# A mixture-of-experts entry on Trainium2: gate weights' low half first, block table later, first down weights beside the first gathers

## What is computed

```python
def hier_moe(x, ...):
    # every token chooses one of 4 groups, and in it 2 of 8 experts, each with a weight
    # pairs (token, weight) are listed by expert; an expert works on blocks of 128 rows
    def expert_block(args):
        xblk, e = args
        hidden = jax.nn.silu(xblk @ w_g[e]) * (xblk @ w_u[e])
        return hidden @ w_d[e]
    # the rows of each block, times their weights, are added to their tokens
```

## Time and profile before

| | us |
|---|---|
| median of 3 runs | 1715.81 (1714.29 to 1717.73) |
| the profiled execution | 1714.82 |
| its span, first to last instruction | 1713.0 |
| TensorE busy | 1665.4 (97%) |
| TensorE's weight loads busy | 1463.1 (85%) |
| VectorE busy | 1264.9 (74%) |
| ScalarE busy | 930.4 (54%) |
| GpSimd busy | 248.8 (15%) |

### The profile page before, as it was taken

One profiled execution on the slowest core, in us unless ns is written; L12 is line 12 of the kernel. 1 busy time (PEld: TensorE's weight loads), 2 busy tenths in 40 slices (PEclk: granted clock), 3 DMA queues, 4 the chain that ended last, 5 costly groups with the idle time before them and its releaser, 6 DMA issues.

```text
span 1713.0 us, 24990 instructions
## 1 busy us (share of the span) xinstructions
PE 1665.4 (97%) x9010; PEld 1463.1 (85%) x9010; DVE 1264.9 (74%) x2101; ACT 930.4 (54%) x1184; POOL 248.8 (15%) x269
## 2 busy tenths in 40 slices
PE   8999999999999999999999999999999999999994
PEld 7999987777999999879998888888888888888882
DVE  5234799986766667655464558999889899889886
ACT  6363121216433344426343337887878778788785
POOL 4100111110000000011001123511111212122111
PEclk9999999999999999999999998999999999999998
DMA  5402223231243233366343339999999999999975
GB/s 203 145 26 75 75 100 107 94 108 57 93 142 105 93 93 93 102 199 214 117 166 129 105 105 373 390 394 380 383 378 384 377 382 371 377 381 381 384 276 221
DMA packets 103171, 367.26 MB, mean 214 GB/s; under 512 B 14628, under 2 KB 58872, under 8 KB 88240
## 3 DMA queue, kind: packets, MB, share of 16 engines
q1 hardware_dynamic: 79824, 308.76, 48.2%
q0 software_dynamic: 23056, 57.36, 10.3%
q10 hardware_dynamic: 208, 0.08, 0.0%
HBM read 326.24 MB, written 61.22 MB: 226 GB/s over the span
## 4 chain that ended last, share of the span: by engine, by line
PE 72%; PEld 15%; DMA 4%; DVE 3%; ACT 2%; issue 2%; DVEq 1%; SPq 0%; ACTq 0%; PEldq 0%; POOLq 0%
PE bank L1069 68%; PEld bank L1069 15%; PE bank L1524 2%; DMA wraw_down<-in_w_expert_down 1%; DMA wraw_up<-in_w_expert_up 1%; PE bank L1548 1%; DMA uo<-in_x_prompt 1%; DVE gwork L2107 1%; PE bank L1441 0%; DMA h_scr<-ybuf,kdT 0%; ACT L1641 0%; PEld bank L1288 0%; DMA s<-in_state_gla 0%; DMA wraw_gate<-h_scr 0%; DVE wraw_gate L2674 0%
## 5 line engine op out<-in xcount | busy, mean ns | idle before, releaser
L2107 DVE TENSOR_TENSOR wL_down<-wraw_down,wH_down 128x1024 fp32r<-128x1024 f32 x140 | 162.0, 1218 | 25.6 <-ACT wH_down L1641 25.1
L2107 DVE TENSOR_TENSOR wL_up<-wraw_up,wH_up 128x2048 fp32r<-128x2048 f32 x72 | 161.6, 2285 | 21.6 <-ACT wH_up L1641 21.6
L2107 DVE TENSOR_TENSOR wL_gate<-wraw_gate,wH_gate 128x2048 fp32r<-128x2048 f32 x72 | 161.7, 2287 | 12.1 <-ACT wH_gate L1641 12.1
L1641 ACT ACTIVATE wH_up<-wraw_up 128x2048 fp32r<-128x2048 f32 x72 | 134.0, 1909 | 66.2 <-DMA wraw_up<-in_w_expert_up 51.8
L2232 DVE SCALAR_TENSOR_TENSOR ybuf<-uo,gwork,ybuf 128x1024 f32<-128x1024 f32 x120 | 154.5, 1288 | 6.1 <-issue 6.1
L1641 ACT ACTIVATE wH_down<-wraw_down 128x1024 fp32r<-128x1024 f32 x140 | 136.6, 1051 | 18.5 <-DMA wraw_down<-in_w_expert_down 18.4
L1641 ACT ACTIVATE stage<-bank 128x512 f32<-128x512 f32 (+3 forms) x65 | 34.5, 546 | 190.2 <-PE bank L1069 180.8
L997 POOL DMA_INDIRECT h_scr<-ybuf,kdT x34 | 77.1, 2269 | 399.7 <-ACT ybuf L1641 360.9
L1641 ACT ACTIVATE wH_gate<-wraw_gate 128x2048 fp32r<-128x2048 f32 x72 | 134.5, 1934 | 1.2 <-DMA wraw_gate<-in_w_expert_gate 1.2
L1069 PE MATMUL bank<-nTH,gateH 128*128 128x352 f32 x384 | 129.5, 337 | 0.7 <-issue 0.6
L1069 PE MATMUL bank<-nTH,slabH 128*128 128x352 f32 x384 | 124.9, 325 | 1.2 <-ACT uo L1641 0.7
(11 more groups left out here) (359 smaller groups left out, 4279.5 us busy)
## 6 DMA issues: line engine op xcount, KB each, us to landing
wraw_gate<-in_w_expert_gate SPq DMA_DIRECT2D x36, 2048.0 KB, 19.1
wraw_up<-in_w_expert_up SPq DMA_DIRECT2D x36, 2048.0 KB
wraw_down<-in_w_expert_down SPq DMA_DIRECT2D x36, 2048.0 KB
slab_raw<-in_w_in SPq DMA_DIRECT2D x7, 2048.0 KB, 9.6
gate_scr<-stage POOLq DMA_DIRECT2D x16, 528.0 KB, 3.6
vr_scr<-stage POOLq DMA_DIRECT2D x32, 256.0 KB, 2.3
gate_raw<-in_w_in SPq DMA_DIRECT2D x16, 512.0 KB, 8.7
vrbuf<-vr_scr SPq DMA_DIRECT2D x16, 512.0 KB, 6.9
```

Source lines behind the costliest of these rows:

```text
L1641: return act.activation(out, in_, func, **kw)
L2107: return dve.tensor_tensor(out, x, y, op)
```

## The change

On SyncE's queue the down weights of block 0 go ahead of the wait for gather 0, and the up weights of block 1 wait for gather 1 too. On VectorE the low halves of block 0 go ahead of the count and the weight list, and the table of further blocks is made after block 2 instead of before block 0; the two steps that take up the table move two blocks later. On TensorE four fillers go ahead of the last token list; sixteen fillers stand between the list and the first transposes (there were two); the weight list and the count come after those transposes, then two fillers (there were eight). On GpSimd, gathers 3 and 4 and scatter 0 go ahead of the table. The loops of TensorE and VectorE begin at block 6 instead of block 4.

```diff
@@ SyncE
             load_w(sp, W_UP, 0, 0)
             load_w(sp, W_GATE, 1, 1)
+            load_w(sp, W_DOWN, 0, 0)
             sp.wait_ge(xg_loaded[0], 16)
-            load_w(sp, W_DOWN, 0, 0)
+            sp.wait_ge(xg_loaded[1], 16)
             load_w(sp, W_UP, 1, 1)
@@ GpSimd
             gather(2)
+            gather(3)
+            gather(4)
+            scatter(0)
             pool.wait_ge(more_made, 1)
...
-            for n in range(NE - 3):
+            for n in range(2, NE - 3):
                 gather(n + 3)
-                if n >= 1:
-                    scatter(n - 1)
+                scatter(n - 1)
@@ TensorE
             ranks(NT - 1)
+            keep_running(4, bk[3])
             pe.wait_ge(slot_made, 2 * NT - 1)
             list_last(tok_hot, 0).then_inc(tok_listed, 1)
-            keep_running(4, bk[3])
-            pe.wait_ge(w_hot_made, NT)
-            list_last(w_hot, NE).then_inc(w_listed, 1)
-            mm(bk[5][:, 0:NE], ones[:, 0:P], macc[:, :], True, True).then_inc(count_ready, 1)
...
             pe.wait_ge(lists_ready, 1)
+            keep_running(16, bk[3])
+            x_block(0, 16)
+            pe.wait_ge(w_hot_made, NT)
+            list_last(w_hot, NE).then_inc(w_listed, 1)
+            mm(bk[5][:, 0:NE], ones[:, 0:P], macc[:, :], True, True).then_inc(count_ready, 1)
             keep_running(2, bk[3])
-            x_block(0, 16)
-            keep_running(8, bk[3])
             block_products(0, 0, 16, None, first=True)
             block_products(1, 1, 32, None)
             block_products(2, 0, 32, None)
+            block_products(3, 1, 48, None)
+            block_products(4, 0, 48, None)
             pe.wait_ge(lists_f, 1)
...
-            block_products(3, 1, 48, None)
-            with pe.Fori(2, NE // 2 - 1) as i:
+            block_products(5, 1, 64, None)
+            with pe.Fori(3, NE // 2 - 1) as i:
@@ VectorE
+            weight_low(W_GATE, 0, 0)
+            x_low(0, 0)
+            weight_low(W_UP, 0, 0)
             dve.wait_ge(count_ready, 1)
             dve.tensor_copy(cnt, bk[5][:, 0:NE])
             dve.wait_ge(w_listed, NT)
             dve.tensor_copy(by_turn(lst_w), in_turns(bk[7][:, NE:2 * NE]))
             dve.drain()
-            weight_low(W_GATE, 0, 0)
-            x_low(0, 0)
-            weight_low(W_UP, 0, 0)
+            dve_block(0, 0, True, None, first=True)
+            dve_block(1, 1, True, None)
+            dve_block(2, 0, True, None)
             dve.wait_ge(const_ready, 7)
...
             dve.tensor_copy(m_int, m_out).then_inc(more_made, 1)
-            dve_block(0, 0, True, None, first=True)
-            dve_block(1, 1, True, None)
+            dve_block(3, 1, True, None)
             dve.wait_ge(listed_rows, 16)
...
-            dve_block(2, 0, True, None)
+            dve_block(4, 0, True, None)
             dve.wait_ge(lists_T, 1)
...
-            dve_block(3, 1, True, None)
-            with dve.Fori(2, NE // 2 - 1) as i:
+            dve_block(5, 1, True, None)
+            with dve.Fori(3, NE // 2 - 1) as i:
```

## The result

**Slower: 1722.59 us** (median of 12 runs, 1717.65 to 1724.53) against 1714.09 for the kernel before on the same chip (12 runs, 1712.52 to 1718.75). The ratio is 1.0039, with a 95% interval of 1.0029 to 1.0048. The prediction was 1713.4 with a range to 1716.3. It was set against the 1715.81 of the first three runs of the kernel before, so it forecast -2.4 us, and +8.5 us came. It was wrong, in sign too.

A forecast was written before the change was run, and what follows sets the result against it. TensorE, 97% busy, was taken as the bound nearly always, with DMA also full. TensorE could gain 0.7 + 1.74 + 0.60 = 3.0 us, transfers allowed 2.4; the smaller held: -2.4 us, 1713.4, range 1710.8 to 1716.3.

The forecast's parts named there:

- The down weights beside the gathers: L = +2 us: Entry: gather 0's landing (L) moves from 1038.2 to 1040.2 beside the down weights, 2 us; ends 0 and 9.5 us.
- one for one: Entry: the gather's packets share evenly with the weights', 27 a us each, instead of 89 alone.
- First product 0.7 earlier: Entry: the first expert product starts at 1042.2 instead of 1042.93, 0.7 us earlier.
- the 1043.5 that the prediction named as a sign of being wrong: Entry: a first expert product starting after 1043.5 would show the prediction wrong.
- The 2.0 us from landing to product: Entry: half the transposes, ScalarE's copy, VectorE's difference and handovers take 2.0 us at full clock after gather 0 lands.
- The fillers: Entry, TensorE: sixteen fillers (32 records) start at half clock, lift it near 1039 to 1040, and end at about 1040.8.
- The stream is 2.4 us ahead, and the lead should last: Weight transfers: by 1042.4 they are 1.05 MB ahead, worth 2.4 us, kept to the end.
- the 1.74 + 0.60 us that the sum counted on: Near the end: TensorE's late stalls, 1.74 us, and the last wait for up weights, 0.60 us, would go.
- Cost 0: Table moved behind block 2: costs nothing on VectorE (uncovered at most 3.4 us), GpSimd or TensorE.
- gather 5 about 2 us later: GpSimd, table moved: gather 5 goes about 2 us later, a block and more ahead of its use.
- Gather 0 is starved: Rival, entry: gather 0 takes 12.8 us, first product at 1050.7, +5.5 us in sum, 1721.3; chance 5%.
- the late stalls' 2.34 us: Near the end: 1.74 us of stalls plus the 0.60 us last wait, counted as gained in the rivals too.

The follow-up runs named there:

- b3: Kernel before with only the first half of block 0's down weights queued ahead of gather 0, the other half behind it: 1718.15 us, ratio 1.0021.
- b2: Kernel before with block 0's down weights and block 1's up weights queued ahead of the gathers, the second down load behind gather 1: 1721.5 us, ratio 1.0038.
- a1: Changed kernel with SyncE's part undone: down weights wait for gather 0 again, block 1's up weights no longer wait for gather 1: 1717.81 us, ratio 1.0011.
- a5: a3 with the gate's low part split around the tokens' low part and VectorE told to wait for the issue of gathers 0 and 1: 1715.79 us, ratio 1.0009.
- a3: Changed kernel with SyncE's part undone and gather 5 put ahead of GpSimd's wait for the table: 1715.94 us, ratio 1.0004.
- a4: a3 with VectorE waiting for gather 0 to land before it makes the gate weights' low half: 1716.2 us, ratio 1.0008.
- d1: Changed kernel with a filler count of 42 instead of 16 ahead of the first transposes: 1719.96 us, ratio 1.0023.
- b1: Kernel before with only SyncE's part: block 0's down weights queued ahead of gather 0, block 1's up weights behind gather 1: 1720.28 us, ratio 1.0025.
- c4: Kernel before with SyncE issuing the down and up loads on GpSimd's increment behind the issue of gathers 0 and 1, not gather 0's landing: 1721.38 us, ratio 1.0043.
- c3: a3 with the gate's low part split and started at gather 0's landing, and SyncE's loads released as in c4: 1723.16 us, ratio 1.0055.
- c1: Changed kernel with a filler count of 68 instead of 16 ahead of the first transposes: 1728.73 us (4 runs), ratio 1.009.
- a2: Changed kernel with gather 5 put ahead of GpSimd's wait for the table: 1721.52 us, ratio 1.0032.

## Why the prediction was wrong

**"The down weights beside the gathers: L = +2 us."** This step failed; the wait was +6.08. It read "one for one" from the earlier trace rows, where 27 packets of GpSimd's queue stood beside 27 of the weights. But those 27 carried 0.00 MB, and they were the slot scatter's: they show that small packets of transfers already under way pass, and nothing about a gather issued behind a queued load. In the changed kernel no row of gather 0 moved for 5.8 us. The row that was nearest in kind is the earlier trace rows, a gather issued behind full queues at 12.8 us. The prediction had it, as the far bound, and set it aside because "only 1.1 MB of weights are left". b3 shows that even 1.05 MB hold it back by 3 us.

The rule of the Trainium skill (DMA: Bandwidth & Descriptors, Queues, rings and completion order) that an engine takes turns between queues packet by packet would have given the same too small figure: in 1036:1037 of the changed kernel GpSimd's queue moved 1 packet against 26. No trace shows whether the gather's packets had reached the engines by then, so this doesn't show the rule broken; once they move, in b2, the trace agrees with it (30 to 31, 32 to 32). The page's memory latency, weighed in the prediction at up to 1.8 us, was too small as well: 2 + 1.8 = 3.8 us against 6.08.

**"First product 0.7 earlier."** VectorE's part of it was right (started 0.8 us after gather 0's issue began, done before the rows came). It came to nothing, since the rows were later than it: the first product started at 1046.03, past the 1043.5 that the prediction named as a sign of being wrong, and 13.6 us after gather 0's issue instead of 8.05. The 2.0 us from landing to product were too few as well. They are 2.2 to 2.6 us at full clock (x(0) to first product in a1, a5 and a3), since the weight list, the count and two fillers on TensorE are not done by then, and 4.2 us in the changed kernel at 0.50.

**What the low half stands beside** had no term. It cost gather 1 its place ahead of the loads: 1.3 to 1.6 us to x(1) in the traces of a1, a3 and a5 (15.15, 14.97 and 15.23 from gather 0's issue, against 13.64). The changed kernel has the 2.59 us issue too, but there both gathers stand behind the down weights anyway, and what the issue costs there was not tried. The Trainium skill (SBUF — State Buffer, Who interferes with whom) says that a VectorE instruction with two inputs in SBUF contends with GpSimd's reads there, but infers that such a subtraction leaves descriptor generation alone. The measurement decides: 2.59 against 1.03 us.

**The fillers.** Predicted to start at half clock and lift it. Which it is changes by execution: in a1 and a4 they did just that (0.50 until 1037.2 and 1037.9) and held the transposes 1.3 to 1.4 us. In the changed kernel's trace they ran at full clock and it fell in the wait behind them: with a gather this late, 32 records are too few. d1 prices this at 3.4 to 4.5 us in the traces (16.93 against 20.28 and 21.44), 2.7 in the median.

**"The stream is 2.4 us ahead, and the lead should last."** Only its start is right: the gate load issued at 1083.6, that of the same block as the one near 1078 in the earlier trace rows, landed in 10.7 us (11.4 before). Near the end one issued at 1621.0 took 24.6 us (24.3 before), and one late period was 19.93 us. The late stalls (periods over 17.75) don't follow the entry: 0.73 + 0.84 = 1.57 us in b1 and 0.62 + 0.75 = 1.37 in c4, both with loads issued earlier than before and TensorE later; 0 in a3 and c3. What sets them stays open. So the 1.74 + 0.60 us that the sum counted on did not come.

**The table: "Cost 0".** Right for VectorE: TensorE waited 0.8 us at most for a hidden low half. Wrong for GpSimd: "gather 5 about 2 us later" was 25 us later, because the text counted what is ahead in the queue and not the wait of the instruction there, 24.41 us for the moved table. The prediction did not name what is queued behind that wait.

**The rivals.** "Gather 0 is starved", at 5%, was the mechanism, and its 1721.3 the nearest number, partly by luck: it took a longer landing (12.8 for 9.4) and counted on the late stalls' 2.34 us, which did not come. 5% was too low for a case whose only "against" was an argument, with a row for it.

## What to carry to other kernels

Before a small transfer is put beside a large one, look for a row in which such a transfer was *issued behind* one, and take its landing as the price, not a packet count from transfers under way. When an operation is moved later, list on every engine the instruction that waits for it and what stands behind that one in its queue. Compare profiles of single executions from an event upstream of the change, or the upstream's own spread (6 us here) is read as the edit's.

## What the runs showed of the hardware

- Gathers 0 and 1, of 128 list entries each, landed 3.3 to 4.6 us after their issue where that issue ended ahead of SyncE's next load; 5.7 and 6.2 us behind half a load; 9.0 to 9.4 behind one; 11.4 and 12.9 behind two (b2); and where the issue ended behind SyncE's issue of the loads, 11.8 to 17.0 (c3, c4, and gather 1 of a1, a3 and a5).
- Near the end of the gate load and the start of the down load queued behind it, packets took 1.6 us each in the changed kernel instead of 0.61, 2.9 in c1, and for 2 to 3 us hardly any queue moved. A load that starts behind a pause begins slowly too: 16 packets of 1.4 us in 1044:1045 of the changed kernel (142.2%), 13 of 2.0 us in 1036:1037 of c4 (163.5%), 12 of 1.1 us in 1039:1040 of the kernel before (83.8%). The cause is open.
- Gather 1's issue on GpSimd took 2.59 to 2.66 us beside VectorE's subtraction with both inputs in SBUF (7 traces), and 1.03 without (9).
- An increment that GpSimd does behind two indirect issues passed 0.36 us after the start of the first one's record, and before the second one's began (c3, c4). It is no sign that the issues are done.
- In an idle wait of 6.4 us TensorE's granted clock fell from 1.00 to 0.50, and it came back only after 9 us of work at half clock (changed kernel); in a2 the wait was 6.2 us and the work at half clock 7 us.
